# Squares, sums, means and roots of all eight row tiles made inside the stick-breaking stage, and a new hand-over to the output projection

## The reference, cut to what matters

```python
y = xf * lax.rsqrt(jnp.mean(xf * xf, axis=-1, keepdims=True) + EPS)      # rms_norm, per head
o_a = merge_heads(rms_norm(o_a) * gla_norm_w[l]) * jax.nn.silu(ga)       # 4 heads of 128
o_b = merge_heads(rms_norm(o_b) * hgrn_norm_w[l]) * jax.nn.silu(gb)      # 4 heads of 64
o_c = merge_heads(stick_breaking_attn(qc, kc, vc)) * jax.nn.silu(gc)     # 4 heads of 64
y = jnp.concatenate([o_a, o_b, o_c], axis=-1) @ w_out[l]
x = x + gate[:, None, :] * y
return rms_norm(x) * final_norm_w
```

```python
between = lax.cumsum(log_1m_beta, axis=3, reverse=True) - log_1m_beta    # log_1m_beta = log_sigmoid(-z)
weights = jnp.where(strict, jnp.exp(log_beta + between), 0.0)            # log_beta = log_sigmoid(z)
outs.append(jnp.einsum('bhts,bhsv->bhtv', weights, v_blk))
```

## Time and profile before

| | us |
|---|---|
| median of 3 runs | 2087.08 (2085.28 to 2090.69) |
| the profiled execution, its own time | 2089.51 |
| its span | 2087.7 |
| PE busy | 2006.0 (96%) |
| VectorE busy | 935.6 (45%) |
| ScalarE busy | 582.0 (28%) |
| GpSimd busy | 375.4 (18%) |

### The profile page before, as it was taken

One profiled execution on the slowest core, in us unless ns is written; L12 is line 12 of the kernel. 1 busy time (PEld: TensorE's weight loads), 2 busy tenths in 40 slices (PEclk: granted clock), 3 DMA queues, 4 the chain that ended last, 5 costly groups with the idle time before them and its releaser, 6 DMA issues.

```text
span 2087.7 us, 37980 instructions
## 1 busy us (share of the span) xinstructions
PE 2006.0 (96%) x15592; PEld 1139.2 (55%) x15592; DVE 935.6 (45%) x1545; ACT 582.0 (28%) x1073; POOL 375.4 (18%) x315
## 2 busy tenths in 40 slices
PE   7999999999998999998999999999999999999997
PEld 6476564766433445453446554565666666666553
DVE  3434553455676753586557674344511111111114
ACT  4123230423674221243123422232111111111113
POOL 0204323324252003005000233000100000000003
PEclk9999999999999999999999999999999999999998
DMA  9221221202525022600030311012999999999986
GB/s 394 81 81 36 96 81 45 77 26 86 172 91 181 30 96 65 168 1 0 0 121 11 141 41 52 12 41 80 354 403 403 405 407 412 410 408 409 404 337 248
DMA packets 104554, 360.51 MB, mean 173 GB/s; under 512 B 20536, under 2 KB 59856, under 8 KB 90128
## 3 DMA queue, kind: packets, MB, share of 16 engines
q1 hardware_dynamic: 58016, 280.37, 34.3%
q0 software_dynamic: 16368, 55.85, 8.1%
q10 hardware_dynamic: 30080, 23.09, 3.4%
HBM read 319.16 MB, written 45.49 MB: 175 GB/s over the span
## 4 chain that ended last, share of the span: by engine, by line
PE 72%; DMA 14%; DVE 8%; ACT 3%; issue 2%; ACTq 1%; POOL 1%; DVEq 0%; POOLq 0%; SPq 0%; PEldq 0%
PE bank L737 18%; DMA y_of_slot<-HT 13%; PE bank L730 13%; PE bank L947 9%; PE bank L1612 8%; PE bank L1628 4%; PE bank L1033 2%; PE bank L973 2%; ACT work L1732 2%; DVE work L2274 1%; PE bank L805 1%; PE bank L1148 1%; DVE O L2274 1%; PE bank L726 1%; DMA slots<-in_w_ada_dram 1%
## 5 line engine op out<-in xcount | busy, mean ns | idle before, releaser
L1732 ACT ACTIVATE work<-bank 128x512 f32<-128x512 f32 (+5 forms) x246 | 123.0, 519 | 346.1 <-PE bank L737 107.5
L1732 ACT ACTIVATE HT<-bank 64x256 f32<-64x256 f32 (+2 forms) x215 | 91.7, 431 | 454.7 <-PE bank L1612 203.8
L1732 ACT ACTIVATE work<-work 128x1024 f32<-128x1024 f32 (+7 forms) x199 | 158.6, 808 | 168.6 <-DVEq L149 114.3
L730 PE MATMUL bank<-slots,HT 128*128 128x512 f32 (+2 forms) x576 | 184.1, 475 | 1.7 <-issue 1.1
L1612 PE MATMUL bank<-slots,HT 128*32 128x256 f32 x3136 | 172.4, 379 | 2.2 <-DVE HT L3112 1.3
L1612 PE MATMUL bank<-work,HT 128*32 128x256 f32 x3072 | 168.7, 379 | 0.0
L3232 POOL TENSOR_TENSOR work<-work 128x1024 f32<-128x1024 f32 (+1 forms) x64 | 111.9, 1748 | 241.8 <-DVEq L149 162.6
L3118 DVE TENSOR_TENSOR HT<-HT,bank 64x256 f32<-64x256 f32 x97 | 41.1, 423 | 246.2 <-ACT HT L1732 245.7
L1612 PEld LDWEIGHTS bank<-slots,HT 128*32 128x32 f32 x3136 | 103.1, 110 | 68.5 <-issue 2.9
L730 PEld LDWEIGHTS bank<-slots,HT 128*128 128x128 f32 x576 | 98.3, 190 | 76.2 <-issue 72.1
L1612 PEld LDWEIGHTS bank<-work,HT 128*32 128x32 f32 x3072 | 101.2, 110 | 64.6
(11 more groups left out here) (348 smaller groups left out, 3109.3 us busy)
## 6 DMA issues: line engine op xcount, KB each, us to landing
slots<-in_w_e_gate_dram SPq DMA_DIRECT2D x17, 2048.0 KB, 12.7
slots<-in_w_e_up_dram SPq DMA_DIRECT2D x17, 2048.0 KB, 17.3
slots<-in_w_e_down_dram SPq DMA_DIRECT2D x17, 2048.0 KB, 17.4
work<-in_w_e_gate_dram SPq DMA_DIRECT2D x16, 2048.0 KB, 12.5
work<-in_w_e_up_dram SPq DMA_DIRECT2D x16, 2048.0 KB, 17.1
work<-in_w_e_down_dram SPq DMA_DIRECT2D x16, 2048.0 KB
slots<-in_w_in_dram SPq DMA_DIRECT2D x8, 2048.0 KB, 9.0
slots<-in_w_ada_dram SPq DMA_DIRECT2D x6, 2048.0 KB, 14.9
```

The costliest lines, as they stand in the source:

```text
L730: ins = pe.matmul(bank, lhsT, rhs, start=(n == 0), stop=(n == len(pairs) - 1))
L1732: return act.activation(o, i, f, bias=bias, scale=scale, **more)
```

## The change

Squares, sums and means of all eight tiles are made in VectorE's queue in the stick-breaking loop: step b gets one of the three parts of tile b // 3, behind `stick_added_up(b - 2)` and ahead of the mask and absolute value of step b + 1. The roots of tiles 0 and 1 are made by ScalarE in step 8, those of tiles 2 to 7 behind step 23; the work on tiles 2 to 7 leaves the projection's loop. `normed_heads(0)` is done before steps 22 and 23 are added up. PE, ScalarE and VectorE announce the end of the stage early and wait for the barrier later; PE runs three idle products, behind its last product, in place of five. ScalarE applies Silu to tile 0's gates apart from tile 1's, without waiting for the barrier, and the stick-breaking gate is applied to tile 0 alone first. GpSimd's sums of weights move to steps 3 to 9 and 13 to 19.

```diff
             return [(j, max(0, (j - 4 * c) * P)) for j in range(4 * c + 4)]
+        SQUARES_AT = range(3 * NT)
+        FIRST_ROOTS_AT = 8
+        WEIGHT_SUMS_AT = (3, 4, 4, 5, 6, 7, 8, 9, 13, 14, 15, 16, 16, 17, 18, 19)
         def totals_before(b):
@@ -1166,15 +1170,17 @@
                         ins = pe.matmul(STICK_OUT[64 * hh:64 * hh + 64, t0:HALF], V[:, j, h * 64:h * 64 + 64],
                                         W[b % 2][hh][:, t0:HALF], start=True, stop=True, skip_group_check=True)
                     ins.then_inc(stick_out, 1)
-            next_phase()
+            pe.wait_ge(stick_exp, 2 * len(SB_STEPS))
+            phases[0] += 1
+            pe.sem_inc(phase, 1)
+            idle_products(stick_bank(len(SB_STEPS) - 3, 0), 3)
+            pe.wait_ge(phase, 4 * phases[0])
             stick_over.append(4 * phases[0])
-            idle_products(banks[7], 5)
             hear("dve")
             turn_tile(0, O[:, 0, :], ringA, SB0 // P)
             turned = [ringA.filled]
-            hear("dve")
             for i in range(NT + 1):
                 if 1 <= i and i + 1 < NT:
                     hear("dve")
                         func(F[n % 2][:, t0:HALF], STICK_TOTALS[:, t0:HALF], ACT.Exp).then_inc(stick_kept, 1)
-            hear("dve")
-            do(rstd[:, 0:16], rstd[:, 0:16], ACT.Ln)
-            do(rstd[:, 0:16], rstd[:, 0:16], ACT.Exp, scale=-0.5)
-            tell("dve")
-            next_phase()
+                if b in (FIRST_ROOTS_AT, len(SB_STEPS)):
+                    hear("dve")
+                    r = rstd[:, 0:16] if b == FIRST_ROOTS_AT else rstd[:, 16:64]
+                    do(r, r, ACT.Ln)
+                    do(r, r, ACT.Exp, scale=-0.5)
+                    tell("dve")
+            act.wait_ge(stick_exp, 2 * len(SB_STEPS))
+            phases[0] += 1
+            act.sem_inc(phase, 1)
             def silu_gates(i0, i1):
                 do(A_GATES[:, :, i0 * P:i1 * P], A_GATES[:, :, i0 * P:i1 * P], ACT.Silu)
...
-            silu_gates(0, 2)
+            silu_gates(0, 1)
+            act.wait_ge(stick_gates_in, 16)
+            do(STICK_GATES[:, 0:4:2, 0:P], STICK_GATES[:, 0:4:2, 0:P], ACT.Silu)
             tell("dve")
-            act.wait_ge(stick_gates_in, 16)
-            do(STICK_GATES[:, 0:4:2, :], STICK_GATES[:, 0:4:2, :], ACT.Silu)
+            silu_gates(1, 2)
+            do(STICK_GATES[:, 0:4:2, P:HALF], STICK_GATES[:, 0:4:2, P:HALF], ACT.Silu)
             tell("dve")
+            act.wait_ge(phase, 4 * phases[0])
             turned_mix(0)
             silu_gates(2, NT)
             do(STICK_GATES[:, 1:4:2, :], STICK_GATES[:, 1:4:2, :], ACT.Silu)
             tell("dve")
             for i in range(NT):
-                if i + 2 < NT:
-                    hear("dve")
-                    r = rstd[:, 8 * i + 16:8 * i + 24]
-                    do(r, r, ACT.Sqrt)
-                    tell("dve")
                 if i + 1 < NT:
...
+            def squared(i):
+                tt(sq, O[:, i, 0:SB0], O[:, i, 0:SB0], ALU.mult)
+            def squares_summed(i):
+                line(dve.tensor_reduce(ssh[:, i, 0:4], cut(sq[:, 0:NG], 4), AX_X, ALU.add))
+                line(dve.tensor_reduce(ssh[:, i, 4:8], cut(sq[:, NG:SB0], 4), AX_X, ALU.add))
+            def means(i):
+                ts(rh[:, i, 0:4], ssh[:, i, 0:4], 1.0 / GLA_DV, EPS, ALU.mult, ALU.add)
+                ts(rh[:, i, 4:8], ssh[:, i, 4:8], 1.0 / HGRN_DV, EPS, ALU.mult, ALU.add)
...
                         .then_inc(stick_logs_done, 1)
                 if b >= 2:
                     stick_added_up(b - 2)
...
-            for i in range(2):
-                mean_squares(i)
-            tell("act")
+                if b in SQUARES_AT:
+                    i, part = divmod(SQUARES_AT.index(b), 3)
+                    (squared, squares_summed, means)[part](i)
+                    if (i, part) in ((1, 2), (NT - 1, 2)):
+                        tell("act")
+            def normed_heads(i):
+                for at, n, dv in ((0, 0, GLA_DV), (NG, 4, HGRN_DV)):
+                    o = cut(O[:, i, at:at + 4 * dv], 4)
+                    tt(o, o, bcast(rh[:, i, n:n + 4].unsqueeze(2), [P, 4, dv]), ALU.mult)
+            hear("act")
+            normed_heads(0)
             for b in range(len(SB_STEPS) - 2, len(SB_STEPS)):
                 stick_added_up(b)
             dve.wait_ge(stick_added, len(SB_STEPS))
-            next_phase()
-            def stick_gated(c):
+            phases[0] += 1
+            dve.sem_inc(phase, 1)
+            def stick_gated(c, first, last):
+                at = slice(first * P, last * P)
                 for pair in range(2):
-                    o = stick_output(pair, c)
-                    tt(o, o, cut(STICK_GATES[:, 2 * pair + c, :], 4), ALU.mult)
+                    o = stick_output(pair, c)[:, first:last, :]
+                    tt(o, o, cut(STICK_GATES[:, 2 * pair + c, at], last - first), ALU.mult)
             def mix_normed(i):
                 if i == 2:
                     hear("act")
-                if i >= 2:
-                    mean_squares(i)
-                    line(dve.reciprocal(rh[:, i, :], rh[:, i, :]))
-                    tell("act")
-                    hear("act")
-                for at, n, dv, gates in ((0, 0, GLA_DV, A_GATES), (NG, 4, HGRN_DV, B_GATES)):
-                    o = cut(O[:, i, at:at + 4 * dv], 4)
-                    tt(o, o, bcast(rh[:, i, n:n + 4].unsqueeze(2), [P, 4, dv]), ALU.mult)
-                if i == 0:
+                if i:
+                    normed_heads(i)
+                if i < 2:
                     hear("act")
                 for at, n, gates in ((0, 4, A_GATES), (NG, 2, B_GATES)):
                     o = cut(O[:, i, at:at + n * P], n)
                     tt(o, o, gates[:, :, i * P:(i + 1) * P], ALU.mult)
-                if i == 4:
-                    stick_gated(1)
+                if i in (0, 1, 4):
+                    stick_gated(*((0, 0, 1), (0, 1, 4), (1, 0, 4))[min(i, 2)])
                 tell("pe")
             hear("act")
             mix_normed(0)
-            hear("act")
-            stick_gated(0)
-            tell("pe")
+            dve.wait_ge(phase, 4 * phases[0])
             mix_normed(1)
...
-                if b == 13:
+                if b == 11:
                     pool.wait_ge(o2_stored, 64)
                     load_rows_of((2, 3))
...
+                for n, at in enumerate(WEIGHT_SUMS_AT):
+                    if at == b:
+                        weight_sums_piece(*divmod(n, 4))
```

More of the change, by code:

```diff
@@ L2574, in stick_added_up @@
                     dve.tensor_copy(o, in_tiles(STICK_OUT)).then_inc(stick_added, 1)
+            ssh, rh = cut(ss, NT), cut(rstd, NT)
+            sq = masks.bitcast(F32)[:, 0:SB0]
+            NG = GLA_HEADS * GLA_DV
+            def squared(i):
[6 more added lines that the diff above has]
+                ts(rh[:, i, 4:8], ssh[:, i, 4:8], 1.0 / HGRN_DV, EPS, ALU.mult, ALU.add)
             for b, (_, _, c, j, t0) in enumerate(SB_STEPS):
@@ L3369, in _ @@
                     pool.tensor_tensor(o, o, in_tiles(F[n % 2][:, t0:HALF]), ALU.mult).then_inc(stick_faded, 1)
-                if b == 13:
+                if b == 11:
                     pool.wait_ge(o2_stored, 64)
                     load_rows_of((2, 3))
-                if 4 <= b < 12 or b >= 16:
-                    weight_sums_piece(*divmod(b - (4 if b < 12 else 8), 4))
+                for n, at in enumerate(WEIGHT_SUMS_AT):
+                    if at == b:
+                        weight_sums_piece(*divmod(n, 4))
             next_phase()
```

## The result

| | before | after |
|---|---|---|
| median of 20 runs | 2085.62 us | 2092.36 us |
| lowest and highest | 2081.72, 2091.39 | 2088.93, 2097.17 |
| profiled execution, its span | 2089.51, 2087.7 | 2093.99, 2091.5 |

The account below looks back on a forecast made before the run. In the stick-breaking stage a VectorE–ScalarE relay without slack was the limit; TensorE was busy nearly all the span. Terms 19.8 - 10.5 - 2.8 = +6.5 us gave 2093.6 us against the median 2087.08; range 2085 to 2102.

Parts of the forecast that it names:

- Pieces in the loop: Stick-breaking loop: squares, sums and means cost 20.0 us, of which 1.4 are hidden in waits for TensorE; net 18.6 slower.
- collisions: Stick-breaking loop: VectorE's pieces meeting GpSimd's products cost between 0 and 13 us; taken as 1.2, one full collision.
- Roots in step 8: ScalarE's roots of tiles 0 and 1, 0.47 us, fit where it waits 0.85 us anyway: no cost.
- End of the stage: From step 23's last L2587 to the projection: 8.6 us in place of 19.1, a gain of 10.5.
- taking the full clock: End of the stage: TensorE's three idle products run at full clock until 5.9 us, and tile 0 is turned at 6.6.
- late next: End of the stage: ScalarE's table load and Silu were named as what is late next.
- The step's bounds, 7 and 11: End of the stage: the gain lies between 7 us (half clock) and 11 us.
- Projection: Projection: TensorE then bounds the tiles; 2.3 us gained by the waits, 3.1 by the period, taken as 2.8.
- The pieces are hidden: Rival, chance 0.08: VectorE's idle 20.4 us in the stage absorbs the pieces; sum -8 to -12 us, about 2077.
- Collisions are the rule: Rival, chance 0.11: in the loop, half of the 13 us of collisions with GpSimd in place of 1.2; about 2099.
- The clock rival: Rival, chance 0.14: TensorE at half clock at the stage's end, +3.5 us, 2097; a spell inside the stage 2 to 3 more.
- the order in time: Stick-breaking loop: a square mostly starts first and GpSimd's product waits; argued for collisions near the lower end.

Follow-up runs that it names:

- e4: The changed kernel with each of the 24 pieces executed twice in a row, at its place; 2123.92 us, ratio 1.0180 over before.
- e7: The changed kernel with only the two reduces of each tile executed twice; 2100.48 us, one execution.
- e1: The changed kernel with the same 24 pieces moved behind their step's absolute values, ahead of L2587; 2077.41 us against before's 2085.52, ratio 0.9954.
- e6: The changed kernel without the three idle products at the end of the stage; 2097.27 us, ratio 1.0065 over before.
- e5: e1 with the pieces cut finer, one half ahead of each L2587 of the step; 2075.27 us against before's 2083.96, ratio 0.9952.
- e8: The changed kernel with only the square of each tile executed twice; 2104.07 us, one execution.

## Why the prediction was right, and where its terms were off

1. *Pieces in the loop (18.6) and collisions (1.2), together 19.8; measured 18.0.* The mechanism held as written: the pieces are not hidden by VectorE's or ScalarE's idle time (after's waits; e4 and e7 one to one; e1, where the same pieces are hidden). The mis-sized term is what hides them after all: the waits for TensorE. I counted two rows of them, 1.4 us; the same view of before has two more, ahead of a mask and of a copy of an output (total us, times, longest):

```profile
DVE bank L2274 <- PE bank L1141: 0.5, 1, 0.5
DVE O L2574 <- PE bank L1166: 0.3, 1, 0.3
```

In all 2.2 us fell to 0.2. The times from the end of one step's last L2587 to the next's, before and after, show where the rest is. An undisturbed square, pair of reduces and pair of tiny operations cost 0.99, 1.16 and 0.41 us, 2.56 a tile and 20.1 for all but tile 7's means. The one collision adds 0.65, a wait for TensorE behind step 14 adds 0.27, and step 5 takes 0.11 more: 21.1. Measured are 18.0, so 3.1 us were hidden, over twice what I took, and all of it in the eight steps in which before waits for TensorE. Behind step 3, for example, where before waits 0.49, the square costs 0.38; behind step 15 (0.32) 0.59; the reduces behind steps 10 and 22 (0.29 each) cost 0.79 and 0.78; the squares behind steps 9 and 21 (0.10 each, left out of the view) 0.79 and 0.78. Those eight waits are 2.3 us, and each piece there saves some 0.1 us beyond the wait. That fits the way that the rows count: an operation of VectorE that waits for nobody starts about 0.09 before the end of the one ahead (567.83 against 567.23 + 0.69 in the earlier trace rows), and a wait is counted from that end on. The collisions came to one of 0.65 us, where I had taken 1.2.

2. *Roots in step 8: nothing.* Right: they start at once behind a ScalarE operation and ScalarE then still waits 0.75 us.

3. *End of the stage, -10.5; measured -8.6.* The term that failed is "taking the full clock": TensorE was at half the clock in its idle products, which ran from 652.63 until 657.9, while VectorE was through at 656.24. That is the 1.5 us of e6's row, or most of the 1.9 missing; VectorE itself was through 7.1 us behind the last L2587, where I had 6.4. In e1 and e5 the clock was at full in the idle products, and there the end took 9.3 and 8.9 us, near the 8.6 of the forecast (tile 7's means stand ahead of the last L2587 in these two, 0.4 us). What I named as late next, ScalarE's table load and Silu, does hold VectorE (its wait of 1.40 us ahead of 654.43). The step's bounds, 7 and 11, held.

4. *Projection, -2.8; measured -4.2.* I averaged 2.3, by the waits, and 3.1, by the period; the period was the right way to count, and its term was too small. TensorE's own work in a tile is 13.73 + 1.53 = 15.26 us, not 15.5: the row of 13.97 that I used is one that follows a wait. Four tiles of 15.26 are 61.0 us in place of 65.1, 4.1 us less, and 65.1 - 61.06 = 4.0 was measured. That TensorE would be the bound of the tiles was right.

5. *The rivals.* "The pieces are hidden" fell: ScalarE's waits grew by 17.7 us. Yet its idle time can be used, as e1 shows, from behind the absolute values. "Collisions are the rule" fell as a price, not as a fact: the squares do meet GpSimd's product, but they start first and GpSimd's product stands, as the order in time had said (1.73 us at 568.91). e4 and e8 show how near it was: a second square starts behind that product and stands itself. The clock rival came true in part, at the end: 1.5 us in the idle products. The first products of tile 0 were at full clock by 660 us, so the other part of its +3.5 did not come. In the stage the clock was at half twice, around 560 and 605 us. The rival had 2 to 3 us for such a spell; the steps, taken apart under 1, leave 0.27 us for it: behind step 14, at 606.88, VectorE waits 0.17 us for TensorE, its only wait for it in the stage. Near 560 us nothing is longer.

The three errors, -1.8, +1.9 and -1.4, partly cancel, so the sum is closer than its terms deserve. That +6.5 met the medians' 6.7 so closely is luck besides: the three stretches give 5.2, and the 1.5 us beyond them stand in none of my terms.

## What to carry to other kernels

In this kernel the idle time of an engine was room only behind the operation that the next engine waits for. In a relay of two engines, put filler work after the hand-over, inside the wait for the answer, not ahead of it. Here the same 24 pieces cost 18 us in the one place and 3 us in the other. Try the parts of a change apart, since one of them may lose more than the other wins. When VectorE work with two SBUF inputs moves, look at what GpSimd does at that moment.

## What the runs showed of the hardware

- TensorE's granted clock fell to half at the end of the stage, between 650.7 and 650.9 us, although its pauses since 640 us had been up to 1.33 us and the one of 1.43 ahead of the last product had only begun at 650.57 (the idle products took 0.88 us a record, 5.29 / 6, where the full clock gives 0.43). The Trainium skill, "TensorE: Matmul & The Clock Gate", in "Part 1: The HAM clock gate (the "warmup" mystery)", ties the throttle to an idle array. Here TensorE had been busy for 38.23 of the 44.2 us before, with short pauses in each step, and it was throttled nonetheless; the prediction had taken from the page that the shorter gap would keep the clock, and the measurement decides. What of this set it off, no run isolates.
- A reduce on VectorE, with one SBUF input, kept its 0.67 to 0.69 and 0.41 to 0.42 us in every kernel, also where squares beside it in the program went from 0.95 to 1.25 on average. The tiny operations (128x4, SBUF to SBUF, one input) were held too: a pair took 1.02 us in place of 0.37, and their mean in e4 was 401 ns against 208. So having one input does not by itself exempt an operation; the section on SBUF cited under e8 has a second condition, a mode of VectorE that uses two ports, and no run here shows which mode these operations ran in.
- Idle products pay although they delay: without them the projection started 1.0 us sooner in absolute time (658.71 against 659.71) but the stage behind the projection started 1.7 us later (658.71 + 124.1 against 659.71 + 121.4).
